# Differential attention heads: modulation multiply-adds one slot later, softmax weighting ahead of the next head's first rounding

## The reference

```python
def diff_attention(xn, positions, w_in, q_gain, k_gain, ..., sub_gain, w_out, layer_idx):
    u = xn @ w_in
    q, k, v, gate = jnp.split(u, 4, axis=-1)
    q = rope(rms_norm(q.reshape(B, S, H, 2, d), q_gain), positions)
    k = rope(rms_norm(k.reshape(B, S, H, 2, d), k_gain), positions)
    ...
        sc = jnp.einsum('bqhcd,bkhcd->bhcqk', q[:, s:e], k[:, :e]) * scale
        sc = jnp.where(chunk_mask(s, e - s, e), sc, -jnp.inf)
        pr = jax.nn.softmax(sc, axis=-1)
        w = pr[:, :, 0] - lam * pr[:, :, 1]
        return jnp.einsum('bhqk,bkhe->bqhe', w, v[:, :e])
    ...
    o = rms_norm(o, sub_gain) * (1.0 - lam_init)
    y = o.reshape(B, S, DA_WIDTH) * jax.nn.silu(gate)
    return y @ w_out

# second block, once for each of its two layers
shift, scale, gate = _adaln(c, ada_w[layer], ada_b[layer])   # c (1, 2048), ada_w (2048, 6144)
h = x * (1.0 + scale) + shift
```

## Time and profile before

| | |
|---|---|
| median of 3 runs | 3611.37 us (3610.76 to 3611.73) |
| the profiled execution | 3606.27 us |
| its span in the profile | 3604.5 us |
| TensorE busy | 3479.2 us, 97% |
| VectorE busy | 2828.2 us, 78% |
| ACT busy | 1937.4 us, 54% |
| GpSimd busy | 588.8 us, 16% |
| granted TensorE clock | full in all of the span |

### The profile page before, as it was taken

How to read it: one execution, slowest core, us unless ns; L and a number is a source line. 1 busy time by engine, 2 the same in 40 slices (tenths; PEclk the granted TensorE clock), 3 DMA queues, 4 the chain that set the end, 5 groups by cost and what they waited for, 6 DMA issues and landing times.

```text
span 3604.5 us, 68495 instructions
## 1 busy us (share of the span) xinstructions
PE 3479.2 (97%) x27986; PEld 3396.4 (94%) x27986; DVE 2828.2 (78%) x4657; ACT 1937.4 (54%) x3076; POOL 588.8 (16%) x546
## 2 busy tenths in 40 slices
PE   7999999999999999999999999999999998999997
PEld 7999999999999999999999999989999898999997
DVE  7777787677787887877787887898989867666665
ACT  6455546566547685565455456554545546434344
POOL 2111112111113011121111112231313310000000
PEclk9999999999999999999999999999999999999999
DMA  6555555534465445655555564445454443555552
GB/s 247 199 212 202 200 234 223 179 152 176 164 269 188 177 164 187 253 184 213 206 202 204 204 257 176 154 151 211 154 212 161 153 162 147 192 208 185 213 188 105
DMA packets 104904, 691.17 MB, mean 192 GB/s; under 512 B 12688, under 2 KB 21008, under 8 KB 22672
## 3 DMA queue, kind: packets, MB, share of 16 engines
q1 hardware_dynamic: 104128, 685.14, 51.2%
q0 software_dynamic: 464, 1.64, 0.1%
HBM read 676.25 MB, written 2.10 MB: 188 GB/s over the span
## 4 chain that ended last, share of the span: by engine, by line
PE 45%; DVE 17%; ACT 6%; issue 3%; POOL 1%; DMA 1%; DVEq 0%; SPq 0%; POOLq 0%; ACTq 0%
PE g L442 13%; PE g L444 13%; PE g L443 13%; DVE w_lo L1568 6%; ACT w_hi L1034 3%; POOL scratch L2392 1%; PE turn_bank L481 1%; DMA scratch<-scratch 1%; DVE scratch L2147 0%; DVE vec L2062 0%; DVE rstd L2062 0%; DVE scratch L2088 0%; DVE sq L2063 0%; DVE con L2100 0%; DVE scratch L2108 0%
## 5 line engine op out<-in xcount | busy, mean ns | idle before, releaser
L1568 DVE TENSOR_TENSOR w_lo<-w_raw,w_hi 128x1024 fp32r<-128x1024 f32 x1088 | 1342.3, 1236 | 450.1 <-ACT w_hi L1034 439.8
L1034 ACT ACTIVATE w_hi<-w_raw 128x1024 fp32r<-128x1024 f32 x1088 | 1128.1, 1053 | 888.4 <-PE g L444 772.4
L442 PE MATMUL g<-p_hi,w_hi 128*128 128x256 f32 x4576 | 1322.3, 289 | 36.9 <-DVE w_lo L1568 23.4
L443 PE MATMUL g<-p_lo,w_hi 128*128 128x256 f32 x4576 | 1297.9, 284 | 0.0
L444 PE MATMUL g<-p_hi,w_lo 128*128 128x256 f32 x4576 | 1297.7, 284 | 0.0
L442 PE MATMUL g<-q_hi,w_hi 128*128 128x256 f32 x3408 | 980.8, 288 | 6.9 <-DVE scratch L2287 2.1
L444 PE MATMUL g<-q_hi,w_lo 128*128 128x256 f32 x3408 | 964.1, 283 | 0.0
L443 PE MATMUL g<-q_lo,w_hi 128*128 128x256 f32 x3408 | 963.8, 283 | 0.0
L442 PEld LDWEIGHTS g<-p_hi,w_hi 128*128 128x128 f32 x4576 | 880.7, 192 | 54.4 <-DVE w_lo L1568 33.5
L443 PEld LDWEIGHTS g<-p_lo,w_hi 128*128 128x128 f32 x4576 | 881.0, 193 | 1.4
L444 PEld LDWEIGHTS g<-p_hi,w_lo 128*128 128x128 f32 x4576 | 880.6, 192 | 0.0
(11 more groups left out here) (451 smaller groups left out, 3988.8 us busy)
## 6 DMA issues: line engine op xcount, KB each, us to landing
w_raw<-in_slots SPq DMA_DIRECT2D x640, 1024.0 KB, 4.9
scratch<-scratch SPq DMA_DIRECT2D x128, 64.0 KB, 4.9
h<-in_x SPq DMA_DIRECT2D x4, 512.0 KB, 6.2
out_h<-h SPq DMA_DIRECT2D x4, 512.0 KB, 2.6
sq<-in_p POOLq DMA_DIRECT2D x4, 256.0 KB, 3.0
con<-in_consts SPq DMA_DIRECT2D x1, 832.0 KB, 10.6
scratch<-in_distance POOLq DMA_DIRECT2D x1, 576.0 KB, 5.4
vec<-in_vecs SPq DMA_DIRECT2D x1, 383.0 KB, 4.1
```

The source lines that it names most:

```text
L442: pe.matmul(g, wh, hi[:, k], start=n == 0, stop=False)
L443: pe.matmul(g, wh, lo[:, k], start=False, stop=False)
L1034: act.activation(w_hi[k % SPLIT][:, cols], raw[MAIN_AT[k] % RAW][:, cols], ACT.Copy).then_inc(hi_ready, 1)
L1568: dve.tensor_tensor(w_lo[k % SPLIT][:, cols], raw[MAIN_AT[k] % RAW][:, cols], w_hi[k % SPLIT][:, cols], SUB).then_inc(lo_ready, 1)
```

## The change

Two moves, both in the differential heads; no instruction is added or taken away.

- The multiply-adds of an ada block move one slot later: from slots 1, 2 and 5, 6 to slots 2, 3 and 6, 7. In slot 7 they stand behind the reductions. The ada load moves one place back in the list of loads.
- In slot 0, `a_silu(1)` and `a_weigh` move from behind the second rounding half to ahead of the first one.

```diff
 def _ada_begins():
...
-    heads = lambda at: [at + 8 * n + m for n in range(A_HEADS) for m in (1, 5)]
+    heads = lambda at: [at + 8 * n + m for n in range(A_HEADS) for m in (2, 6)]
...
         def a_head(y, i, prev, first, jl):
             for j in range(8):
+                if j == 0 and prev:
+                    a_silu(1)
+                    a_weigh(jl)
                 begin()
                 g = take(columns=j == 1 and prev)
...
-                if j == 0 and prev:
-                    a_silu(1)
-                    a_weigh(jl)
...
-                if j in (1, 2, 5, 6):
-                    ada_half([acc[:]], (j - 1) % 4)
+                if j in (2, 3, 6, 7):
+                    ada_half([acc[:]], (j - 2) % 4)
```

## The result

The changed kernel took 3616.76 us, the median of 13 runs (3609.58 to 3625.82). The kernel before, run beside it, took 3610.65 us (13 runs, 3602.81 to 3612.45). The ratio is 1.0024 with a 95% interval of 1.0015 to 1.0032: it is slower by 0.24%, or 8.7 us by the ratio and 6.1 us between the medians. The prediction was 3614 us and +2.7 us. The time lies in its own range of 3607 to 3618 us; the change is just beyond the 0.2% within which I had put most of my chance.

The account below looks back on a forecast made before the run. TensorE was taken as the bound, busy 97% of the span, so VectorE changes count only where it waits. Removed waits (-18.7, -5.1) against new column waits (12 x 1.4, 1.5, 2 x 4.1) gave +2.7 us: 3614, range 3607 to 3618.

Parts of the forecast that it names:

- The waits that go: TensorE in the differential heads: 18.7 us before the weights' transposes and 5.1 us before the scores vanish, 23.8 us together.
- What makes them go: Slot 0: weighting placed ahead of the first rounding means the transposes never wait for it, 18.7 us gained.
- The new wait: Modulation columns wait for the last multiply-add, ending at 188.85 in the sample head: 1.4 us there.
- The clamp on GpSimd: Slot 6: clamp no longer overlaps the rotation's first product, saving 0.2 us; were it to stay, 2.8 us over 14 heads.
- The cover in slot 4: VectorE's idle time before slot 4's second rounding hides the multiply-adds moved into slot 3, by 0.2 us.
- The twelve ordinary boundaries: Heads 1 to 6 of both layers: columns wait as in the sample head, 12 x 1.4 us.
- The first heads: First head of each layer: columns wait 0.75 us, 1.5 us for both layers.
- The last heads: Last head of each layer: less TensorE work before the columns, so a 4.1 us wait each, 8.2 us.
- three loads in a row: Slower rival: slot 4's copy takes 8.5 us, slot 5's lands at 6 to 6.5; 3627 to 3634 us; chance 0.23.
- the upper bound: Slot 5's copy taking 7.0 us, the longest of any copy: waits 58.5 us, +34.7, 3646 us.
- The copy is not the limit: Faster rival: VectorE gains the whole 2.07 us in slot 5; 3596, or 3604 with half; both faster rivals together 0.14.
- The new wait is cheap: Faster rival: sums ready for the columns except in last heads, 15.6 us gained, 3596 us; both faster rivals together 0.14.

Follow-up runs that it names:

- weigh_only: Kernel before with only the weighting moved ahead of slot 0's first rounding; 3593.07 us, ratio 0.9951.
- adds_only: Kernel before with only the multiply-adds moved one slot later, to slots 2, 3, 6, 7; 3615.70 us, ratio 1.0017.
- copy_first: Changed kernel with SP issuing a slot's crosswise copies ahead of the weight load that waits for the same slot's rounding; 3594.11 us, ratio 0.9961.
- first_only: Changed kernel with the second block of multiply-adds put back to slots 5 and 6, the first kept in 2 and 3; 3590.18 us, ratio 0.9946.
- slot7_front: Changed kernel with slot 7's multiply-adds ahead of the silu product, scores and reductions instead of behind them; 3604.18 us, ratio 0.9982.
- last_new: `weigh_only` with the multiply-adds moved one slot later in the last head of each layer alone; 3602.20 us, ratio 0.9978.
- weigh_copy: `weigh_only` with SP issuing a slot's crosswise copies ahead of the weight load, as in `copy_first`; 3586.15 us, ratio 0.9932.
- last_old: Changed kernel with the last head of each layer left at slots 1, 2, 5, 6 for the multiply-adds; 3602.73 us, ratio 0.9980.

## Why the prediction was right or wrong

**The waits that go: right in size.** 23.8 us were to go; 23.4 went.

**What makes them go: wrong.** The prediction put the 18.7 us down to the weighting's new place. `weigh_only` shows that this place is enough, but `adds_only` shows that the wait at the columns removes them as well. The sum did not suffer, because it set all the old waits against all the new ones: for the total that was luck. Read part by part, it makes the weighting's move worth 18.7 us within this change; it was worth nothing measurable there.

**The new wait: right, by its own working.** The predicted end of the last multiply-add was 188.85 on the clock of the kernel before. These are the rows of VectorE in the sample head, to be compared with the earlier trace rows:

```profile
174.03 0.88 DVE L1769 TENSOR_TENSOR scratch<-scratch,sin_a 128x256 f32<-128x256 f32 x1 [0.23 <-DMA scratch<-scratch]
...
179.45 0.42 DVE L1769 TENSOR_TENSOR scratch<-scratch,sin_a 128x256 f32<-128x256 f32 x1 [0.89 <-DMA scratch<-scratch]
...
180.25 2.04 DVE L1633 SCALAR_TENSOR_TENSOR acc<-w_raw,tiny,acc 128x256 f32<-128x256 f32 x4
...
189.25 0.48 DVE L1635 SCALAR_TENSOR_TENSOR acc<-w_raw,tiny,acc 128x256 f32<-128x256 f32 x1
...
189.77 0.42 DVE L1715 TENSOR_TENSOR scratch<-scratch 128x256 f32<-128x256 f32 x1
```

The last one ends at 189.73. The head began 1.02 us later than before (transposes at 143.00 against 141.98), so that is 188.71. Slot 5's copy took 5.0 us as assumed; slot 4's took 7.4 where I had 7.3, and slot 5's rotation waited 0.23 us for it. Slot 6's waited 0.89 (predicted 1.2). The clamp on GpSimd starts at 177.63 and not beside the rotation's first product, which took 0.42 us in place of 0.62, as predicted. The weighting (189.77) follows the multiply-adds at once, as predicted. The cover in slot 4 held: the second rounding there still waited 0.23 us for ACT.

**The twelve ordinary boundaries**: predicted 1.4 us each, 16.8. They lie between 0.84 and 2.08 and sum to 15.0; nine are 0.84 to 1.27 and three 2.07 or 2.08. So the sum agrees better than its terms do. The three are the heads in which slot 6's rotation waited longest for slot 5's copy: 2.39, 2.32 and 2.10 us, where the other nine had 0.38 to 0.93. The first of them:

```profile
340.67 0.43 DVE L1769 TENSOR_TENSOR scratch<-scratch,sin_a 128x256 f32<-128x256 f32 x1 [2.39 <-DMA scratch<-scratch]
```

Its copy's second half was issued at 334.39, so it landed 6.3 us later and not 5.0. Taking every head like the sample hid this. **The first heads**: predicted 0.75 each (the rows give 80.63 - 79.94 = 0.69); 1.83 and 0.69. **The last heads**: predicted 4.1 each; 3.96 and 3.78.

**The step that failed is one that is not there.** The sum turned waits of TensorE into time one for one. In the stretch behind five of the sixteen waits the matmuls ran in part at the lower clock, and that cost 9.4 us, nearly all of the gap between +2.7 and the +11.4 of the profiled execution; by the ratio the gap is 6.0 us. The kernel before has no wait of 2 to 4 us in these heads, but it has such waits elsewhere, and drops of the clock beside them at 1.5 us each. I had taken the clock to be full everywhere and did not look. A rival "a wait of 4 us slows what comes after it" could have been stated and priced, and the last heads, which I had called the place where it costs, were where to put it: they cost 12.7 us and not 8.2.

**The rivals.** The slower one, three loads in a row, came about in part: slot 4's copy landed in 7.4 us in the sample and not 8.5, but slot 5's landed 6.0 to 6.3 us after issue, as that rival had it, in three of the twelve ordinary heads. Slot 4's copies were not late in those three, so the backlog is not the reason; what it is stays open. Nor is it exact that a small copy cannot pass the loads ahead of it: in the trace of the kernel before, the first half of a copy landed ahead of the load issued just before it in about half of 48 cases, the second half never. And the earlier trace rows are those of the first halves alone; second halves took up to 7.6 us, so the upper bound was not the worst case. "The copy is not the limit" fell with the 0.89 us wait, and `copy_first` shows what it would have given. "The new wait is cheap" fell with the 0.69 to 2.08 us in the fourteen heads that are not last. The time fell inside the range, above the forecast, mainly for a reason that none of the rivals had.

**Nothing of this is a large effect on the total.** Between executions of one kernel the time varies by 6 to 16 us, and the mean clock with it (the changed kernel: 0.992 at 3609.6 us, 0.988 at 3625.8). The bookkeeping above is that of single executions; it is the ratios that decide. I set the waits and drops of each kernel's profile against those of the kernel before and compared the sum with the ratio. The kernels whose columns don't wait in ordinary heads come out within 1.4 us of it: `weigh_only` -17.5 against -17.7, `first_only` -18.9 against -19.5, `slot7_front` -5.2 against -6.5, `last_new` -8.6 against -7.9, `weigh_copy` -23.4 against -24.5. The four whose columns wait in every head are all faster than their sum: the changed kernel +11.3 against +8.7, `adds_only` +10.2 against +6.1, `copy_first` -9.9 against -14.1, `last_old` -2.1 against -7.2. The gap is 2.6 to 5.1 us, and the traces settle a part of it. By the start of the last transposes of the heads, against 2032.81 in the kernel before, the changed kernel was 9.7 us late, `adds_only` 8.5 late, `copy_first` 10.4 ahead and `last_old` 4.0 ahead. So by the end of the heads the sums are already 0.5 to 1.9 us too high. The other 1.0 to 3.7 us are left between one execution and the median of many, and one profile of each kernel can't tell what they are. The same traces show what a single span is worth: behind the heads, where all these kernels do the same work, their spans differ from that of the kernel before by -5.4 (`last_old`) to +6.3 us (`weigh_only`).

## What to carry to other kernels

A piece of work moved later to end one wait can become the last thing before its own consumer. So price its move at the consumer, with the iteration that has the least other work before it (here the last head: 4 us where most others had 1). Where two parts of a change act on the same pair of engines, don't add their gains: a new wait upstream may remove an old one downstream by itself, and each part has to be tried alone. And look at the queue before the arithmetic: two copies of 64 KB issued ahead of a 1 MB load instead of behind it gave, with one digit, what moving sixteen multiply-adds a head did not. Before a wait is priced at its length, look in the trace of before for waits as long, and for the clock behind them.

## What I had not expected of the hardware

A wait of TensorE can cost more than its length. Behind the longer waits the granted clock was found at its lower level, 1.2 GHz, for a part of the next microseconds, though TensorE was then busy without a gap. In the changed kernel this took 1.5 us behind three waits of 1.83 to 2.08 us and 2.5 us behind each of the two longest; in `last_new` it took 1.3 us behind waits of 3.85 and 3.80 us. The cost goes with the time that the clock stays down. In `last_new` and behind the three shorter waits that was about 3.4 us. At the two longest of the changed kernel it was twice that, and began before the wait had ended:

```profile
458.50:465.30 6.80, 6.23 (x29) 6.23 (x30) 3.75 (x9) 1.40 (x3) 0.00 (x0) 0.50 0.74 289
```

The wait's length alone does not decide it. In `adds_only` the columns at 1762.76 waited 2.07 us, and the transposes came 6.74 us later, at the full clock:

```profile
1762.76 0.60 PE L517 MATMUL g<-con,acc 128*128 128x1 f32 x4 [2.07 <-DVE acc L1635]
...
1769.50 0.49 PE L481 MATMUL turn_bank<-con,scratch 128*128 128x128 f32 x3
```

The same boundary of the changed kernel waited 2.08 us and took 8.23. In `last_old` the sample head waited only 1.29 us and took 8.22:

```profile
187.69 0.61 PE L517 MATMUL g<-con,acc 128*128 128x1 f32 x4 [1.29 <-DVE acc L1635]
...
195.91 0.49 PE L481 MATMUL turn_bank<-con,scratch 128*128 128x128 f32 x3
```

In all eight waits over 3.1 us (two each in the changed kernel, `adds_only`, `copy_first` and `last_new`), columns to transposes took longer; of the nine between 1.83 and 2.08 us in the changed kernel, `adds_only` and `last_old` it did so behind seven; of the shorter ones, behind two (1.29 and 1.37 us). One of the seven, 2.07 us long in `last_old`, cost 3.0 us: 9.76 us from columns to transposes. What decides whether the clock falls, and for how long, these runs don't tell.
